# A two-layer three-branch encoder on one core: softmax weights of the third branch turned by VectorE in 32x32 blocks and a trip through DRAM

## The reference

```python
h = rms_norm(x, norm_g)
proj = h @ w_in                          # queries, keys, values, gates of all three branches
o_a = gated_linear_attention(...)        # 4 heads, chunks of 64 tokens, both directions
o_b = differential_attention(...)        # 4 heads, softmax(q1 k1) - lam * softmax(q2 k2)
o_c = dilated_window_attention(...)      # 8 heads of 64, three window patterns merged by their log sums
y_n = norm(o_n) * silu(gate_n)           # the third branch without the norm
x = x + (sum_n sigmoid(merge_n) * (y_n @ w_branch_n)) @ w_out
```

## Time and profile before

| | |
|---|---|
| median of three runs | 1236.12 us (1236.11 to 1238.03) |
| the profiled execution | 1238.5 us, its span 1236.7 us |
| granted clock of PE, mean | 0.998 |
| PE busy | 98% of the span |
| POOL, DVE, ACT busy | 67%, 56%, 36% |
| transfers | 148.63 MB, mean 120 GB/s |
| one group in the steady state | 120.6 us (the same piece of PE's work starts at 284.94 and 405.57 us) |

### The profile page before, as it was taken

How to read it: one execution, slowest core, us unless ns; L and a number is a source line. 1 busy time by engine, 2 the same in 40 slices (tenths; PEclk the granted TensorE clock), 3 DMA queues, 4 the chain that set the end, 5 groups by cost and what they waited for, 6 DMA issues and landing times.

```text
span 1236.7 us, 17755 instructions
## 1 busy us (share of the span) xinstructions
PE 1214.0 (98%) x5892; PEld 989.1 (80%) x5892; DVE 698.0 (56%) x1045; ACT 439.8 (36%) x800; POOL 831.4 (67%) x598
## 2 busy tenths in 40 slices
PE   7999999999999999999999999999999999999997
PEld 5887787788878887788888778887888788777886
DVE  6685228632753375677558742474258335748753
ACT  6424523452354245200253353245314531450011
POOL 5787377737763877678749762975388548856881
PEclk9999999999999999999999999999999999999999
DMA  6333233323332333374234332523252315335622
GB/s 241 103 113 111 103 102 102 115 94 102 109 105 93 117 96 119 128 271 153 90 138 136 91 117 71 160 86 105 76 169 84 112 61 153 96 108 206 223 81 69
DMA packets 53136, 148.63 MB, mean 120 GB/s; under 512 B 6880, under 2 KB 10464, under 8 KB 52704
## 3 DMA queue, kind: packets, MB, share of 16 engines
q1 hardware_dynamic: 30144, 103.04, 24.8%
q10 hardware_dynamic: 22944, 44.98, 11.9%
HBM read 114.45 MB, written 16.78 MB: 106 GB/s over the span
## 4 chain that ended last, share of the span: by engine, by line
PE 91%; DVE 4%; ACT 1%; issue 1%; DMA 1%; ACTq 1%; POOLq 0%; POOL 0%; DVEq 0%
PE proj L1137 52%; PE proj L1241 10%; PE turn L1378 4%; PE turn L1302 3%; PE score L1378 3%; PE mbank L1310 2%; PE score L1294 2%; PE obank L1310 2%; PE score L1295 2%; PE mbank L1378 2%; PE obank L1378 2%; PE proj L1155 1%; PE mbank L1129 1%; DVE yl L1048 1%; PE obank L1331 1%
## 5 line engine op out<-in xcount | busy, mean ns | idle before, releaser
L433 POOL TENSOR_TENSOR wl<-raw_w,wh 128x512 fp32r<-128x512 f32 x352 | 504.8, 1454 | 31.7 <-POOL wh L424 31.7
L424 POOL TENSOR_SCALAR wh<-raw_w 128x1024 fp32r<-128x1024 f32 x176 | 213.6, 1214 | 287.0 <-issue 102.1
L1137 PE MATMUL proj<-hh,wh 128*128 128x512 f32 x1016 | 402.4, 396 | 3.3 <-DVE group L941 2.8
L1137 PE MATMUL proj<-hh,wl 128*128 128x512 f32 x1016 | 397.3, 391 | 0.0
L1137 PE MATMUL proj<-hl,wh 128*128 128x512 f32 x1016 | 396.4, 390 | 0.0
L1137 PEld LDWEIGHTS proj<-hh,wh 128*128 128x128 f32 x1016 | 190.8, 188 | 44.4 <-issue 4.9
L1137 PEld LDWEIGHTS proj<-hh,wl 128*128 128x128 f32 x1016 | 190.7, 188 | 41.2
L1137 PEld LDWEIGHTS proj<-hl,wh 128*128 128x128 f32 x1016 | 191.0, 188 | 38.8
L544 ACT ACTIVATE six<-big 128x512 f32<-128x512 f32 x23 | 14.4, 626 | 198.1 <-DVE big L1075 198.1
L964 DVE CUSTOM_DVE_ANT_0 six<-score,lmask 128x512 f32<-128x512 f32 x64 | 43.2, 683 | 69.1 <-PE score L1295 69.1
L729 ACT ACTIVATE big<-turn 128x512 f32<-128x512 f32 x96 | 56.2, 594 | 69.4 <-PE turn L1302 68.9
(11 more groups left out here) (239 smaller groups left out, 1918.2 us busy)
## 6 DMA issues: line engine op xcount, KB each, us to landing
raw_w<-weights SPq DMA_DIRECT2D x175, 512.0 KB, 3.3
gate_scratch<-gstage ACTq DMA_DIRECT2D x48, 256.0 KB, 2.1
six<-gate_scratch ACTq DMA_DIRECT2D x16, 768.0 KB, 5.0
big<-big ACTq DMA_DIRECT2D x64, 128.0 KB, 3.7
yh<-yh ACTq DMA_DIRECT2D x64, 128.0 KB, 2.4
big<-x_t SPq DMA_DIRECT2D x4, 512.0 KB, 6.6
big<-x_t SPq DMA_DIRECT2D x1, 2048.0 KB, 8.8
x_scratch<-big SPq DMA_DIRECT2D x1, 2048.0 KB, 7.3
```

The source lines that it names most:

```text
L424: pool.tensor_scalar(wh[:, slot, :, :], src, 1.0, 1.0, ALU.mult, ALU.mult).then_inc(pool_high.sem, 1)
L433: ins = pool.tensor_tensor(wl[:, slot, half, :], src[:, half, :], wh[:, slot, half, :].bitcast(F32), ALU.subtract)
L1137: last = pe.matmul(dst, a[:, slot, k, :], b[:, k, :], start=(k == 0 and a is wh and b is hh), stop=(k == KT - 1 and a is wl))
```

## The change

Six of the eight third-branch units, 4 to 9, are no longer turned by PE. The list `VIA` names them, and `BY_PE` the six that PE still turns. For a unit in `VIA`:

- DVE makes only the reciprocal (`inverse`), and ACT multiplies the tile by it in place (`scale`);
- DVE turns the tile within 32x32 blocks (`turn_32`) into half of a pair's buffer: pairs 0 and 2 use `w`, pair 1 uses `group[:, 8:10]`;
- when both units of a pair are there, SP stores the buffer to DRAM with one transfer of 128 x 16 runs of 64 numbers, 512 KB in all (`send`), waits for it, and reads it back with four transfers of 128 KB (`bring`), each to 32 partitions of `wt1` or `wt`;
- PE waits for all three pairs (`back`) before the group's last product.

The weights now lie pair by pair: in a pair's 256 columns the two query blocks alternate every 32 columns. So the product's columns come out in that order, and DVE's last multiplication by the gate is six pieces of 64x128 and one of 64x256 in place of one of 128x512. The third branch's scores are made head by head instead of block by block. Units 10 and 11 are scaled by DVE in `probs` and turned by PE as before. PE's filling steps are dealt out anew, the first group's three steps ahead of `scores(0)` among them, and `lambda_scales` of the first group (four small operations on DVE) stands before the wait for the swapped halves instead of after the low parts.

```diff
 BRANCH_TILE, OUT_TILE = 1 + NG * NT, 1 + NG * NT + 24
+VIA = list(range(4,10))
+BY_PE = [u for u in range(12) if u not in VIA]
...
+        def paired(t):
+            return t.rearrange("p k s -> p (k s)").rearrange("p (m k e) -> p m k e", m=2, k=QB)
+        def pair_buffer(m):
+            return group[:, 8:10, :] if m == 1 else w
...
+        def w_free(G, u):
+            if u in VIA:
+                m = VIA.index(u) // 2
+                return sent[m - 2].at(G, 16) if m >= 2 else turn_done.at(G, len([n for n in BY_PE if n < u]))
+            return turn_done.at(G, BY_PE.index(u - 2) + 1)
...
+            def send(G, m):
+                sp.wait_ge(*turned_32.at(G, 2 * m + 2))
+                sp.dma_start(turned_d[m, :, :, :].rearrange("x p j -> p x j"), pair_buffer(m)[:, :, :].rearrange("p n s -> p (n s)").rearrange(
+                    "p (x j) -> p x j", j=64)).then_inc(sent[m].sem, 16)
+            def bring(G, m):
+                u = VIA[2 * m]
+                if u == 4:
+                    sp.wait_ge(*c_parts.at(G, 1))
+                    apart(sp)
+                sp.wait_ge(*sent[m].at(G, 16))
+                if u == 8:
+                    sp.wait_ge(*out_done.at(G, 3))
+                    apart(sp)
+                weights = paired(wt1 if u < 8 else wt)
+                for c in range(4):
+                    sp.dma_start(weights[32 * c:32 * c + 32, u % 4 // 2, :, :].rearrange("i k (a j) -> i (k a) j", j=64),
+                                 turned_d[m, QB * c:QB * c + QB, :, :].rearrange("x (a i) j -> i (x a) j", i=32)).then_inc(back.sem, 16)
...
+                        if j == 15:
+                            send(L * NG + i, 0)
+                    send(L * NG + i, 1)
+                    bring(L * NG + i, 0)
+                    send(L * NG + i, 2)
+                    bring(L * NG + i, 1)
+                    bring(L * NG + i, 2)
...
+                    def scale(u):
+                        j = 2 * u if u < 4 else u + 4
+                        act.wait_ge(*rs_ready.at(G, VIA.index(u) + 1))
+                        act.activation(probs[:, j % 4, :], probs[:, j % 4, :], ACT.Copy, scale=rs[:, j:j + 1]).then_inc(scaled.sem, 1)
...
-                    for u in range(4, 10):
-                        exp(u + 6)
-                        turned(u)
-                        if u == 5:
-                            merge_gate(2)
-                            act.wait_ge(*out_done.at(G, 2))
-                            grp.did(act.activation(rr[:, 0, :], mbank[:, :], ACT.Ln, bias=cst[:, 0:1]))
...
-                            act.activation(rr[:, :, :], rr[:, :, :], ACT.Exp, scale=-0.5).then_inc(r_done.sem, 1)
-                        if u == 7:
-                            merge_gate(3)
-                        if u == 9:
...
+                    scale(4)
+                    exp(10)
+                    scale(5)
+                    exp(11)
+                    merge_gate(2)
+                    scale(6)
+                    exp(12)
+                    scale(7)
+                    exp(13)
+                    scale(8)
+                    scale(9)
+                    act.wait_ge(*out_done.at(G, 2))
+                    grp.did(act.activation(rr[:, 0, :], mbank[:, :], ACT.Ln, bias=cst[:, 0:1]))
...
+                    grp.did(act.activation(rr[:, 1, :], obank[:, :], ACT.Ln, bias=cst[:, 0:1]))
+                    grp.last()
+                    act.activation(rr[:, :, :], rr[:, :, :], ACT.Exp, scale=-0.5).then_inc(r_done.sem, 1)
+                    merge_gate(3)
+                    exp(14)
+                    exp(15)
                     turned(10)
+                    merge_gate(4)
                     turned(11)
                     merge_gate(5)
...
                     for t, m in ((qhat, 0), (cum, 1), (rest, 1)):
                         ins = dve.tensor_tensor(t, raw[:, m, :], t, ALU.mult)
                     ins.then_inc(a_read.sem, 1)
+                    if first:
+                        lambda_scales()
...
                             grp.last()
-                            dve.tensor_scalar(w[:, u % 2, :], probs[:, j % 4, :], rs[:, j:j + 1], None, ALU.mult).then_inc(w_ready.sem, 1)
+                            dve.tensor_scalar(probs[:, j % 4, :], probs[:, j % 4, :], rs[:, j:j + 1], None, ALU.mult).then_inc(w_ready.sem, 1)
...
+                        else:
+                            j = u + 4
+                            dve.wait_ge(*exp_done.at(G, j + 1))
+                            dve.reciprocal(rs[:, j:j + 1], sums[:, j:j + 1]).then_inc(rs_ready.sem, 1)
+                    def turn_32(u):
+                        j = 2 * u if u < 4 else u + 4
+                        dve.wait_ge(*scaled.at(G, VIA.index(u) + 1))
...
+                        if u >= 2:
+                            dve.wait_ge(*w_free(G, u))
+                        dve.transpose(by_quarter(pair_buffer(VIA.index(u) // 2)[:, :, :], u % 2), probs[:, j % 4, :].rearrange("p (k c j) -> p k c j", k=QB, c=4)).then_inc(turned_32.sem, 1)
...
                         if u == 1:
                             silu(2, "cg")
-                    weights(4)
+                    inverse(4)
                     row_max(10)
+                    turn_32(4)
                     dve.wait_ge(*sq_done.at(G, 2))
                     dve.wait_ge(*sq_high_done.at(G, 2))
                     dve.tensor_tensor(sq_low, sqb[:, :], sq_high.bitcast(F32), ALU.subtract).then_inc(sq_low_done.sem, 1)
                     dve.scalar_tensor_tensor(y[:, NG + i, :], obank[:, :], sc[:, 4:5], sg[:, 1, :], ALU.mult, ALU.mult).then_inc(y_read.sem, 1)
-                    for u in range(5, 12):
-                        weights(u)
-                        if u < 10:
-                            row_max(u + 6)
-                        if u == 8:
-                            dve.wait_ge(*r_done.at(G, 1))
-                            dve.wait_ge(*y_read.at(G, 2))
-                            grp.did(dve.tensor_tensor(y[:, i, :], y[:, i, :], rr[:, 0, :], ALU.mult))
-                            dve.tensor_tensor(y[:, NG + i, :], y[:, NG + i, :], rr[:, 1, :], ALU.mult).then_inc(ab_normed.sem, 1)
+                    inverse(5)
+                    row_max(11)
+                    turn_32(5)
+                    inverse(6)
+                    row_max(12)
+                    row_max(13)
+                    turn_32(6)
+                    inverse(7)
+                    turn_32(7)
+                    inverse(8)
+                    inverse(9)
+                    row_max(14)
+                    turn_32(8)
+                    row_max(15)
+                    turn_32(9)
+                    dve.wait_ge(*r_done.at(G, 1))
+                    dve.wait_ge(*y_read.at(G, 2))
+                    grp.did(dve.tensor_tensor(y[:, i, :], y[:, i, :], rr[:, 0, :], ALU.mult))
+                    dve.tensor_tensor(y[:, NG + i, :], y[:, NG + i, :], rr[:, 1, :], ALU.mult).then_inc(ab_normed.sem, 1)
+                    weights(10)
+                    weights(11)
                     dve.wait_ge(*out_done.at(G, 5))
-                    dve.scalar_tensor_tensor(y[:, 2 * NG + i, :], mbank[:, :], 0.5, sg[:, 2, :], ALU.mult, ALU.mult).then_inc(y_read.sem, 1)
+                    h0, h1 = rows_of(0), rows_of(1)
+                    for b in range(QB):
+                        dve.scalar_tensor_tensor(tokens(y[h0, 2 * NG + i, :], b), by_token(mbank[h0, :], b), 0.5, tokens(sg[h0, 2, :], b), ALU.mult, ALU.mult)
+                    for b in range(2):
+                        dve.scalar_tensor_tensor(tokens(y[h1, 2 * NG + i, :], b), by_token(mbank[h1, :], b), 0.5, tokens(sg[h1, 2, :], b), ALU.mult, ALU.mult)
+                    t = slice(2 * P, 4 * P)
+                    dve.scalar_tensor_tensor(y[h1, 2 * NG + i, t], mbank[h1, t], 0.5, sg[h1, 2, t], ALU.mult, ALU.mult).then_inc(y_read.sem, 1)
...
-                            last = pe.transpose(turn[u % 2][:, P * k:P * k + P], w[:, u % 2, P * k:P * k + P], ident[:, :])
+                            part = w[:, u % 2, P * k:P * k + P] if u < 4 else probs[:, u % 4, P * k:P * k + P]
+                            last = pe.transpose(turn[u % 2][:, P * k:P * k + P], part, ident[:, :])
...
-                    if first:
-                        fill(3)
                     scores(0)
                     fill(4)
                     scores(1)
...
-                    values(4, out_done, (obank[:, :], slice(P, 2 * P), wt))
-                    for u in range(4, 10):
-                        if u % 2 == 0:
-                            scores(u // 2 + 3)
-                        fill(3 if u in (5, 7) else 4)
-                        turn_weights(u)
-                        if u == 5:
-                            pe.wait_ge(*y_read.at(G, 2))
-                            mean_of(obank, 2)
+                    pe.wait_ge(*wt_ready.at(G, 4))
+                    values((obank[:, :], slice(P, 2 * P), [wt[:, k, :] for k in range(QB)]))
```

(16 more changed lines are left out.)

90 lines of the change are left out of this document (58 added, 32 removed).

## The result

The changed kernel takes 1229.28 us (median of 4 runs, 1227.65 to 1230.89) against 1236.46 (1236.11 to 1238.03) on the same chip: 0.9936 of it, interval 0.9924 to 0.9948. It is faster, by 7.2 us. The forecast was 1219, a gain of 17. The profiled execution took 1229.05 us, its span 1226.9 (before 1236.7, so 9.8 less; the kernel before was profiled in an execution 2.4 us above its median, so the difference of the spans is larger than that of the medians).

The account below looks back on a forecast made before the run. PE was taken to bound the kernel (91% of the chain that ended last). Turns -21.1, first groups -2.3, layer ends +3.9, handovers +2.4 sum to -17.1 us, carried to the median 1236.12: 1219, range 1212 to 1245.

Parts of the forecast that it names:

- the transfers: Pair 2's store, issues and load landing before a group's last product: 9.6 us of 11.3 available, so no wait.
- the 0.2 of handovers: Allowance of 0.2 us for handovers within the 9.6 us path of pair 2's store and loads.
- 32 ns: Price of one 256-byte packet on a DMA engine, from a line through two queues' rows; 4.1 us a store.
- The 48 turns by PE: Six units in eight groups leave PE, 0.44 us for each turn: 21.1 us less.
- The first groups: Each layer's first group: filling steps moved, two PE waits gone; 0.1 us gained in layer one, 2.2 in two: -2.3.
- The end of a layer: DVE's last multiplication in seven pieces takes 1.95 us more, exposed at two layer ends: +3.9 us.
- Handovers: Thin margins of DVE and ACT for PE around the third-branch turns: 0.3 us a group charged, +2.4.
- the anchor: Start of the new path's timing: at 479.2, the second score tile's maximum ahead of turn 4 starts.
- the third rival: ACT or DVE becomes the bound: 1 to 2 us a group, 1227 to 1235; chance 0.20 together with rival one.
- the first, transfers partly late: Weights land up to 2.3 us late a group, up to 1237; between 1223 and 1234, 0.20 with the third.
- The second: Short runs cost more than any row says: slower, 1254 or 1296; 0.22 together with the first rival's far end.
- its first threshold, 5.0: Store time in us above which pair 2 also waits for pair 0's store, so each further us counts twice.

Follow-up runs that it names:

- the first experiment: The changed kernel with SP issuing pair 2's store ahead of pair 0's loads instead of behind them; 1234.39 us, 0.9985 of the kernel before.

## Why the prediction failed

**The step that failed** is the transfers: "4.9 + 1.5 + 3.0 + 0.2 = 9.6, so the weights are back 1.7 us before PE asks". It counted, behind the end of pair 2's turn, a store, three issues and one landing, and nothing for the eight loads of pairs 0 and 1 that stand ahead in the same queue and use the same DMA engines. By the rows of the steady group, the changed kernel's and those of the kernel that loads pair 2 only:

| from the end of pair 2's second turn | forecast | only pair 2 loaded | changed kernel |
|---|---|---|---|
| until the store is issued | in the 0.2 of handovers | 0.0 | 1.9 (365.56 to 367.45) |
| store to pair 2's first load issue | 4.9 | 4.2 | 5.5 (to 372.92) |
| three issues | 1.5 | 1.6 | 1.4 (to 374.35) |
| the last load's landing | 3.0 | 3.3 | 3.8 (to 378.20) |
| sum | 9.6 | 9.1 | 12.6 |
| until PE asks | 11.3 | 11.9 | 11.9 |

The path's own sum was right within half a microsecond, the store faster and the load slower than priced; the eight loads beside it, priced at nothing, add 3.5 us where 2.7 were free. The largest difference is the wait behind pair 0's loads, whose issues run from 363.47 to 367.33, the first alone 2.15 us. That it isn't a simple matter of order is shown by the first experiment.

Two things set the last landing. *Issues:* with bytes alike and packets within 1%, 24 instead of 15 a group cost 13.9 us of waits. *Transfers in flight:* with SP's issues alike, four loads on the other queue take the landing of pair 2's last load from 2.8 to 5.2 us in the steady group and the waits from none to 6.1 us. Whether their packets or their bytes do it isn't shown: no run changed the number of packets alone. Runs of 1 KB in the loads instead of 256 bytes, with 15 issues in both, bring the waits from 7.5 to 2.6, but the split of issues changes too (12 stores and 3 loads against 3 and 12), and the engines' time hardly falls. Nor did a run move ACT's gate store or the next group's weight rows, which are in flight with the last load.

The forecast had the means for the second: its own 32 ns times 12,288 packets over 16 engines are 24.6 us of full DMA engines in a stretch of about 20. Even at the 18.4 ns estimated from the two traces they are 14.1, before any weight row (the share measured from 358.40 to 378.20 was 0.96). Packets were counted there for the landing of single transfers only.

**The 48 turns by PE** (-21.1): right. They are 192 turns instead of 384, and in the kernels whose loads are left out, the steady group takes 118.2 to 118.4 us (374.61 to 492.83 with only pair 2 loaded), 2.4 less than 120.6, as forecast.

**The first groups** (-2.3): the number came out, by luck. The kernel with only pair 2 loaded shows it, where no load is waited for. In the first layer 0.6 us is gained (forecast 0.1): the first product comes at 137.98 instead of 140.95, 3.0 sooner, of which the turns and the handover are 2.4. Both old waits are gone, and the wait for DVE's sum is there with 1.8 (1.7 in the changed kernel, forecast 2.1). In the second layer, where 2.2 were to be gained, 0.8 is lost: from the last product of the first layer to the first of the second are 241.0 us instead of 241.4, 0.4 less, where the turns alone give 2.4 and the end of the layer takes 1.2. There the scores wait 0.85 (numbers of the changed kernel) for the copies of `yh`, and 0.8 for `w` and 0.9 for an exponential follow in the same group. Two of these waits are not new. Before, they stood in the second group of the first layer, for which nothing was forecast:

```profile
214.92 0.66 PE L1302 MATMUL turn<-ident,w 128*128 128x128 f32 x4 [0.72 <-DVE w L998]
221.83 0.50 PE L1294 MATMUL score<-yh 128*128 128x512 f32 x1 [0.99 <-ACT six L721]
```

That group took 123.0 us from product to product (140.95 to 263.97), 2.4 more than the groups behind it, and takes 118.3 now, the steady time. Together -2.1. Why the waits moved stays open.

**The end of a layer** (+3.9): the mechanism is right, the size is half. It measured 1.2 us a layer against before and 1.05 against the single operation, +2.1 to 2.4.

**Handovers** (+2.4, 0.3 a group): 0.23 a group, all at unit 10, where DVE's multiplication takes 0.89 us. The turn by blocks takes 0.71 us and the next operation starts 0.63 after it, 0.62 forecast; pair 2 was ready 11.9 us after the anchor (353.71 to 365.56), 12.1 forecast. So the third rival did not occur.

**Sum on the span**: -21.1, -2.1, +2.4, +1.8 give -19.0, beside the -18.9 measured with only pair 2 loaded (1236.7 to 1217.8) and the forecast's -17.1. In the changed kernel the waits for the loads put 7.5 back and the wait at 17.66 another 0.9, and -10.6 stands beside the measured -9.8. The medians moved less than the spans, -16.1 and -7.2. The kernel before was profiled 2.4 us above its median, and 2.4 is also what its second group took too long; with one trace of it, whether that is the same 2.4 stays open, and with it whether the forecast was right to carry the difference over to the median.

**The rivals.** It is the first, transfers partly late (1223 to 1237, between 1223 and 1234 for 0.20 with the third), by another way than written there: with the store near the middle of its bounds, not at the upper end, and the loads late by what stands ahead of and beside them. The second did not occur: at x = 4.5 to 4.7 the store is under its first threshold, 5.0, if only just (in the steady group pair 0's took 5.03 and landed at 363.45, 0.2 us before the turn that waits for it), and the 18.4 ns of a short packet lie below the 32 that were to be doubled. Chances and range held the result (1229 in 1212 to 1245), the predicted time did not.

The sign was therefore right for the reason given, and less than half of the gain came, since a new wait took it.

## What to carry to other kernels

When work goes to a detour through DRAM, add up the whole queue and not the last transfer's own chain: all issues in order with what each waits for, and all that is in flight beside them, and compare that with the time until the reader asks. Storing a pair in four pieces, so that it comes back in one plain load, was worth more here (6.6 us) than any change of the order or of the queue (5.1 and 23.7 us lost, 2.4 won). What the transfers beside the path cost is cheap to find by a kernel that leaves them out: it gave the forecast's time to 1.2 us, and the difference to the full kernel is their price.
